# A fourth seven-product pair in the first down trip of each chunk, with its weight sums made at the end of up

## The chip, the cores and the metric

One core of one Trainium2 chip runs the whole kernel in one launch. The metric is the device time of one execution in microseconds (us). Each version is timed in several runs and the median is given.

## The reference, cut to what matters

A decoder layer: a token-mixing sub-layer with three branches, then a squared-ReLU MLP, on 256 tokens of 2048 channels, all float32. The change touches only the MLP, and there only its second matrix product:

```python
D_MODEL, SEQ, D_FF = 2048, 256, 4 * 2048
h = rmsnorm(x, norm_ffn_g[l])
x = x + jnp.square(jax.nn.relu(h @ w_up[l])) @ w_down[l]
return rmsnorm(x, final_g)
```

## The kernel before

**Precision.** Each float32 weight is split in a high part `w_hi` (made by ScalarE, L607) and a low part `w_lo` = weight - high (VectorE, L890), and so are the activations. A product is then three matmuls: high x high, low x high, high x low.

**Slabs.** Weights stream from memory in slabs of 512 KB, 128x1024 elements. SyncE issues the loads into 8 raw buffers (`w_raw`). The split forms lie in a ring of 4 (`w_hi`, `w_lo`). In step k of the program ScalarE and VectorE prepare slab k + 3 while TensorE multiplies slab k.

**Chunks.** The MLP is cut in 4 chunks of 2048 hidden channels. A chunk is the phase `up` (4 trips of 8 slabs; a trip has two groups n = 0 and 1 of 4 slabs, so the trip's last step is k = 7) and the phase `down` (2 trips of 16 slabs; the two groups n = 0 and 1 are two blocks of 512 output columns, i = 0 to 7 is the place along the hidden channels). Chunk 0 and chunk 3 are written out, chunks 1 and 2 are a loop.

**The end of a group of up.** When a group's last slab has been multiplied, ScalarE copies half of the sums out of PSUM (`second`, L816), VectorE adds the other half (L1438), multiplies by the row scale (L1440, which counts the semaphore `evac_done`), squares the ReLU (L1487), and after the last step of a trip also makes four sums of activations for the seven-product form (`a_sums`, L961 to L966) and the low parts (L1493, L970). Group n uses the PSUM banks 4 + 2n and 5 + 2n, and so does group n of `down`. Therefore the first slab of a group of down (i = 0) waits until the group of up that held the same banks has been taken out:

```python
if i == 0:
    pe.wait_ge(evac_done, g - 1)
```

**Seven products in place of eight.** Two slabs with the same i, (0, i) and (1, i), hold a 2x2 arrangement of weight blocks. Multiplied plainly they take 2 x 12 matmuls of 512 columns (`products_as`, L1559 to L1561). As a Strassen-Winograd product (`products_quad`, L1608 to L1610) they take 7 x 3 = 21. This needs four sums of weight blocks, made by VectorE in `forms_first` (one instruction of 128x1024, L901) and `forms_second` (two of 128x512, L908, L911), their high parts by ScalarE (`forms_hi`, two of 128x1024, L613, L615) and their low parts by VectorE (`forms_lo`, two of 128x1024, L917). In return one block of the second slab needs no split of its own: only half of it is split (L605, L887). The sums of activations for i = 1, 3, 5, 7 are all made at the end of the four up trips (`a_forms[0]` to `[3]`); before the change a_forms[0] is made and not used in down.

**The order.** `order_of` gives the order of slabs in a trip, `quads` says at which steps a seven-product pair begins: (6, 10, 14). The sums of the pair at step q are made in step q - 4 (`forms_first`), q - 3 (`forms_second`), q - 2 and q - 1 (high and low parts). Each engine runs its instructions in the order of the program; within a step of VectorE that order is `forms_second`, `lo`, `forms_first`, `forms_lo`, then the end of a group. `walk` says which trips are loops.

Of the kernel before, what the change touches and what calls it, by code (L numbers as in the profile page):

```python
# [51 lines left out]
LOOKAHEAD = 3  # L52
# [4 lines left out]
KDOWN = D // DROWS  # L57
# [43 lines left out]
PH = plan()  # L101
# [7 lines left out]


PAIR = [(0, 0), (0, 1), (1, 0), (1, 1), (0, 2), (1, 2), (0, 3), (1, 3), (0, 4), (1, 4), (0, 5), (1, 5)]
PAIR_ENDS = {False: [(0, 6), (1, 6), (0, 7), (1, 7)], True: [(0, 6), (0, 7), (1, 6), (1, 7)]}
P_BANK = {"P1": 0, "P6": 1, "P7": 2, "P5": 3}
T1, T3, T2, T4 = range(4)
# [2 lines left out]
MIX_QUADS, GATE_QUADS = 3, 6  # L117
# [3 lines left out]
def last_trip(ph, c, t):  # L121

    return ph.name == "down" and isinstance(c, int) and c == CHUNKS - 1 and isinstance(t, int) and t == ph.trips - 1
# [6 lines left out]
def opening(ph, c, t):  # L130

    return ph.name == "glu" and isinstance(t, int) and t == 0


def order_of(ph, c, t):

    if opening(ph, c, t):
        return [(n, i, KFULL) for n, i in OPENING]
    if ph.name == "A":
        return [(n, i, KDOWN) for n, i in PAIR + PAIR_ENDS[False]] + ph.slabs[16:]  # L140
    if not (ph.name == "down" or ph.name == "mix" and t == 0):
        return ph.slabs
    return [(n, i, KDOWN) for n, i in PAIR + PAIR_ENDS[last_trip(ph, c, t)]]


def quads(ph, c, t):

    if ph.name == "A" or ph.name == "mix" and t == 0:
        return (6, 10, 14)
    if ph.name != "down":  # L150
        return ()
    return (6,) if last_trip(ph, c, t) else (6, 10, 14)


def quad_of(ph, c, t, k):

    at = quads(ph, c, t).index(k)
    if ph.name == "A":
        return t * 3 + at
    return GATE_QUADS + at if ph.name == "mix" else c * (3 * PH["down"].trips) + t * 3 + (at + GATE_QUADS + MIX_QUADS)  # L160


def pair_of(ph, c, t):
# [11 lines left out]
def trip_behind(ph, c, t):  # L175

    if ph.name in ("mix", "down") and t:
        return ph, c, t - 1
    if ph.name == "up" and isinstance(t, int) and not (isinstance(c, int) and c == 0):
        return PH["down"], c - 1, PH["down"].trips - 1  # L180
    return None

# [26 lines left out]
WARM_GAP = 3  # L209


def walk(eng, body):

    def loop(name, c=0, first=0):
        with eng.Fori(first, PH[name].trips) as t:
            body(PH[name], c, t)

    body(PH["glu"], 0, 0)
    loop("glu", first=1)
    for t in range(PH["short"].trips):  # L220
        body(PH["short"], 0, t)
    body(PH["kv"], 0, 0)
    for t in range(PH["q"].trips):
        body(PH["q"], 0, t)
    body("v tokens", 0, 0)
    for t in range(PH["B"].trips):
        body(PH["B"], 0, t)
    for t in range(PH["C"].trips):
        body(PH["C"], 0, t)
    for t in range(PH["A"].trips):  # L230
        body(PH["A"], 0, t)
    for t in range(PH["mix"].trips):
        body(PH["mix"], 0, t)
    def chunk(c):
        body(PH["up"], c, 0)
        loop("up", c, first=1)
        for t in range(PH["down"].trips):
            body(PH["down"], c, t)

    chunk(0)  # L240
    with eng.Fori(1, CHUNKS - 1) as c:
        chunk(c)
    chunk(CHUNKS - 1)
# [21 lines left out]
def build(nc, x, norm_mix_g, w_in, gate_b, conf_dw, conf_ln_g, conf_ln_b, w_conf_out, sconv_w,  # L265
# [5 lines left out]
    with ctx:  # L271
# [123 lines left out]
        t_raw, t_two, t_hi, t_lo = sem("t_raw"), sem("t_two"), sem("t_hi"), sem("t_lo")  # L395
# [46 lines left out]
        def half_rows(slab, a):  # L442

            return wide_rows(slab)[:, a, :]
# [146 lines left out]
        def _(act):  # L591
            def hi(ph, c, t, k):

                s = slab_of(ph, c, t, k)
                if isinstance(s, int) and s + LOOKAHEAD >= TOTAL:
                    return
                ahead = k + LOOKAHEAD

                raw = raw_slot(ph, t, ahead)
                act.wait_ge(raw_full[raw], raw_count(ph, c, t, ahead))  # L600
                if not (isinstance(s, int) and s == 0):
                    act.wait_ge(slab_used, s)
                q = ahead % RING
                if ahead - 1 in quads(ph, c, t):
                    act.activation(half_rows(w_hi[:, q], 1), half_rows(w_raw[:, raw], 1), ACT.Copy).then_inc(hi_done, 1)  # L605
                else:
                    act.activation(w_hi[:, q], w_raw[:, raw], ACT.Copy).then_inc(hi_done, 1)  # L607

            def forms_hi(ph, c, t, k):

                if k + 2 in quads(ph, c, t):
                    act.wait_ge(t_raw, quad_of(ph, c, t, k + 2) * 2 + 2)
                    act.activation(forms_of(ph)[:, 0, 2:4, :], w_sums[:, 2:4, :], ACT.Copy).then_inc(t_hi, 1)  # L613
                if k + 1 in quads(ph, c, t):
                    act.activation(forms_of(ph)[:, 0, 0:2, :], w_sums[:, 0:2, :], ACT.Copy).then_inc(t_hi, 1)  # L615

            def first_product(ph, c, t, k):
# [250 lines left out]
                        if k == 12:  # L868
                            closing_squares()

            walk(act, trip)
            act.wait_ge(rstd3, 2)
            act.wait_ge(y_gain, 2 * NBLK)
            act.activation(yg_tok[:, 1, W2:], yg_tok[:, 1, W2:], ACT.Copy, scale=tok_stat[:, 2, 1:2]).then_inc(scaled[3], 1)
# [3 lines left out]
        def _(dve):  # L878
            def lo(ph, c, t, k):
                s = slab_of(ph, c, t, k)  # L880
                if isinstance(s, int) and s + LOOKAHEAD >= TOTAL:
                    return
                q, raw = (k + LOOKAHEAD) % RING, raw_slot(ph, t, k + LOOKAHEAD)

                dve.wait_ge(hi_done, s + (LOOKAHEAD + 1))
                if k + LOOKAHEAD - 1 in quads(ph, c, t):
                    dve.tensor_tensor(half_rows(w_lo[:, q], 1), half_rows(w_raw[:, raw], 1),  # L887
                                      half_rows(w_hi[:, q], 1).bitcast(F32), ALU.subtract).then_inc(lo_done, 1)
                else:
                    dve.tensor_tensor(w_lo[:, q], w_raw[:, raw], w_hi[:, q].bitcast(F32), ALU.subtract).then_inc(lo_done, 1)  # L890

            def forms_first(ph, c, t, k):

                x, y = raw_slot(ph, t, k), raw_slot(ph, t, k + 1)
                quad = quad_of(ph, c, t, k)
                if not (isinstance(quad, int) and quad == 0):
                    dve.wait_ge(t_lo, quad * 2)
                dve.wait_ge(raw_full[x], raw_count(ph, c, t, k))
                dve.wait_ge(raw_full[y], raw_count(ph, c, t, k + 1))
                left = w_raw[:, x:x + 2, 0:2, :].rearrange("p s k b -> p s (k b)")  # L900
                dve.tensor_tensor(w_sums[:, T1:T3 + 1, :], wide_rows(w_raw[:, y]), left, ALU.subtract).then_inc(t_raw, 1)  # L901

            def forms_second(ph, c, t, k):

                x, y = raw_slot(ph, t, k), raw_slot(ph, t, k + 1)
                quad = quad_of(ph, c, t, k)
                dve.wait_ge(t_raw, quad * 2 + 1)
                dve.tensor_tensor(w_sums[:, T2, :], half_rows(w_raw[:, y], 1), w_sums[:, T1, :],  # L908
                                  ALU.subtract).then_inc(t_two, 1)
                dve.wait_ge(t_two, quad + 1)  # L910
                dve.tensor_tensor(w_sums[:, T4, :], half_rows(w_raw[:, x], 1), w_sums[:, T2, :],  # L911
                                  ALU.subtract).then_inc(t_raw, 1)

            def forms_lo(ph, c, t, k, part):
                dve.wait_ge(t_hi, quad_of(ph, c, t, k) * 2 + part + 1)
                two = slice(2, 4) if part == 0 else slice(0, 2)
                dve.tensor_tensor(forms_of(ph)[:, 1, two, :], w_sums[:, two, :], forms_of(ph)[:, 0, two, :].bitcast(F32),  # L917
                                  ALU.subtract).then_inc(t_lo, 1)
# [369 lines left out]
            def trip(ph, c, t):  # L1288
# [4 lines left out]
                for k in range(ph.nslabs):  # L1293
# [10 lines left out]
                    if opening(ph, c, t) and k == 5:  # L1304
# [1 line left out]
                        dve.reciprocal(mix_stat[:, 3, :], mix_stat[:, 2, :]).then_inc(inv1, 1)  # L1306
                        dve.wait_ge(inv1, 1)
                        spread_diagonal(diag1)
                    if k + 3 in quads(ph, c, t):
                        forms_second(ph, c, t, k + 3)  # L1310
                    if k == 15 and paired(ph, c, t) and ph.name != "A":
                        corner_sums(ph, c, t)
                    lo(ph, c, t, k)
                    if k == 0 and trip_behind(ph, c, t):
                        token_sums(*trip_behind(ph, c, t))
                    if k + 4 in quads(ph, c, t):
                        forms_first(ph, c, t, k + 4)
                    if k + 2 in quads(ph, c, t):
                        forms_lo(ph, c, t, k + 2, 0)
                    if k + 1 in quads(ph, c, t):  # L1320
                        forms_lo(ph, c, t, k + 1, 1)
                    n, i, size = order_of(ph, c, t)[k]
                    s, g, ends = slab_of(ph, c, t, k), group_of(ph, c, t, n), i == size - 1
                    if ph.name == "down" and not last_trip(ph, c, t):
# [10 lines left out]
                    if opening(ph, c, t):  # L1335
# [10 lines left out]
                        if k == 6:  # L1346
# [3 lines left out]
                            n, i, size = order_of(ph, c, t)[5]  # L1350
# [39 lines left out]
                    if ph.name == "short":  # L1390
# [4 lines left out]
                        first = sum(CONV_SHORT[m] for m in range(k))  # L1395
# [26 lines left out]
                    if ph.name == "C":  # L1422
                        at = t * ph.nslabs + k
# [79 lines left out]
                            dve.tensor_tensor(y_tok[:, b, cols], acc[:, bank(ph, n) + b, :], y_tok[:, b, cols],  # L1503
                                              ALU.add).then_inc(done, 1)

            walk(dve, trip)


        @block.tensor
# [356 lines left out]
```

## Time and profile before

| | |
|---|---|
| median of 3 runs | 1507.08 us (1505.09 to 1507.33) |
| the profiled execution, its own time | 1505.21 us |
| its span in the trace | 1503.4 us |
| TensorE busy | 1491.5 us, 99% of the span |
| VectorE busy | 1246.7 us, 83% |
| ScalarE busy | 780.2 us, 52% |
| DMA engines | 61.1% |
| granted TensorE clock | 0.999 |

The span is what the trace covers; some 1.8 us of the execution's own time lie around it. TensorE is busy in the whole span, so the end moves with what TensorE has to do and with what it has to wait for.

### The profile page before, as it was taken

The page shows a single profiled execution, that of the slowest core. Times are in us where ns is not written, and L with a number is a line of the kernel's source. Part 1 is how long each engine was busy: PE and PEld are TensorE (multiplying, and loading weights), DVE is VectorE, ACT ScalarE, POOL GpSimd, SP SyncE. Part 2 cuts the span into 40 slices and gives each one's busy share as a digit, 9 for nine tenths or more (in the row PEclk, how much of TensorE's full clock was granted, in tenths as well). Part 3 has the DMA queues.
Part 4 walks back from the last instruction along what each step waited for, and adds up shares of the span by engine and source line. Part 5 has one row for each costly group of instructions (what it writes and reads, how often), then busy time and mean ns, then how long its engine had stood idle before and what let it go on. Part 6 is the DMA issues. An engine that isn't in the chain of part 4 may idle for free.

```text
span 1503.4 us, 21159 instructions
## 1 busy us (share of the span) xinstructions
PE 1491.5 (99%) x7574; PEld 1260.7 (84%) x7574; DVE 1246.7 (83%) x1670; ACT 780.2 (52%) x979; POOL 2.0 (0%) x11
## 2 busy tenths in 40 slices
PE   8999999999999999999999999999999999999998
PEld 7888888888888888888888888888888888888886
DVE  6668889988889879998976779977898779987897
ACT  6444444465554456556565455545555545544554
POOL 0000000000000000000000000000000000000000
PEclk9999999999999999999999999999999999999999
DMA  9666665665556666665655656655666566656662
GB/s 310 194 184 188 193 195 183 204 185 177 177 175 198 194 192 197 207 215 185 195 185 182 195 173 217 205 191 171 210 201 205 168 206 204 194 180 209 209 203 90
DMA packets 210028, 291.11 MB, mean 194 GB/s; under 512 B 9276, under 2 KB 129156, under 8 KB 209827
## 3 DMA queue, kind: packets, MB, share of 16 engines
q1 hardware_dynamic: 209954, 290.14, 61.1%
q8 instruction: 45, 0.74, 0.2%
q14 instruction: 29, 0.23, 0.0%
HBM read 287.48 MB, written 2.10 MB: 193 GB/s over the span
## 4 chain that ended last, share of the span: by engine, by line
PE 99%; DVE 0%; ACT 0%; DMA 0%; issue 0%; SPq 0%; DVEq 0%
PE acc L1539 27%; PE acc L1559 14%; PE acc L1560 14%; PE acc L1561 14%; PE acc L1537 13%; PE acc L1609 3%; PE acc L1608 3%; PE acc L1610 3%; PE acc L1532 2%; PE acc L1636 1%; PE acc L1534 1%; PE acc L1702 0%; PE acc L1722 0%; PE acc L1580 0%; PE acc L1579 0%; PE acc L1578 0%
## 5 line engine op out<-in xcount | busy, mean ns | idle before, releaser
L607 ACT ACTIVATE w_hi<-w_raw 128x1024 fp32r<-128x1024 f32 x502 | 524.5, 1057 | 437.5 <-PE acc L1561 237.2
L890 DVE TENSOR_TENSOR w_lo<-w_raw,w_hi 128x1024 fp32r<-128x1024 f32 x502 | 605.8, 1221 | 139.4 <-ACT w_hi L607 135.7
L1539 PE MATMUL acc<-h_hl,w_hi 128*128 128x512 f32 x1740 | 546.6, 395 | 0.0
L1537 PEld LDWEIGHTS acc<-h_hl,w_lo 128*128 128x128 f32 x1740 | 322.3, 188 | 73.1 <-issue 0.7
L1537 PE MATMUL acc<-h_hl,w_lo 128*128 128x256 f32 x1740 | 343.5, 279 | 0.4 <-DVE w_lo L1044 0.3
L1539 PEld LDWEIGHTS acc<-h_hl,w_hi 128*128 128x128 f32 x1740 | 265.2, 189 | 0.0
L1559 PE MATMUL acc<-w_hi,m_hl 128*128 128x512 f32 x424 | 165.3, 390 | 0.0
L1560 PE MATMUL acc<-w_lo,m_hl 128*128 128x512 f32 x424 | 165.0, 389 | 0.0
L1561 PE MATMUL acc<-w_hi,m_hl 128*128 128x512 f32 x424 | 165.0, 389 | 0.0
L1559 PE MATMUL acc<-w_hi,h_hl 128*128 128x512 f32 x336 | 132.2, 394 | 0.0
L1561 PE MATMUL acc<-w_hi,h_hl 128*128 128x512 f32 x336 | 130.9, 389 | 0.0
L1560 PE MATMUL acc<-w_lo,h_hl 128*128 128x512 f32 x336 | 130.8, 389 | 0.0
L1098 DVE SCALAR_TENSOR_TENSOR conv<-glu,par,conv 128x256 f32<-128x256 f32 x240 | 108.9, 479 | 1.4
L1561 PEld LDWEIGHTS acc<-w_hi,m_hl 128*128 128x128 f32 x424 | 79.6, 188 | 16.5
L1559 PEld LDWEIGHTS acc<-w_hi,m_hl 128*128 128x128 f32 x424 | 79.6, 188 | 16.5
L1560 PEld LDWEIGHTS acc<-w_lo,m_hl 128*128 128x128 f32 x424 | 79.6, 188 | 16.4
L816 ACT ACTIVATE second<-acc 128x512 f32<-128x512 f32 x58 | 34.7, 599 | 101.7 <-PE acc L1539 101.7
L1438 DVE TENSOR_TENSOR pair<-acc,second 128x512 f32<-128x512 f32 x54 | 37.2, 690 | 54.4 <-ACT second L816 54.3
L1559 PEld LDWEIGHTS acc<-w_hi,h_hl 128*128 128x128 f32 x336 | 63.1, 188 | 14.1 <-issue 1.3
L1561 PEld LDWEIGHTS acc<-w_hi,h_hl 128*128 128x128 f32 x336 | 63.1, 188 | 13.3
L1560 PEld LDWEIGHTS acc<-w_lo,h_hl 128*128 128x128 f32 x336 | 63.1, 188 | 12.7
L917 DVE TENSOR_TENSOR w_forms<-w_sums,w_forms 128x1024 fp32r<-128x1024 f32 x50 | 60.9, 1219 | 0.0
(270 smaller groups left out, 1651.8 us busy)
## 6 DMA issues: line engine op xcount, KB each, us to landing
w_raw<-in_w_in SPq DMA_DIRECT2D x197, 512.0 KB, 4.3
w_raw<-in_w_up SPq DMA_DIRECT2D x128, 512.0 KB, 4.3
w_raw<-in_w_down SPq DMA_DIRECT2D x128, 512.0 KB, 4.5
w_raw<-in_w_mix_out SPq DMA_DIRECT2D x32, 512.0 KB, 3.9
w_raw<-in_w_sconv_out SPq DMA_DIRECT2D x16, 512.0 KB, 3.8
w_raw<-in_w_attn_out SPq DMA_DIRECT2D x16, 512.0 KB, 3.8
w_raw<-in_w_conf_out SPq DMA_DIRECT2D x16, 512.0 KB, 4.0
bias_row<-in_gate_b SPq DMA_DIRECT2D x10, 256.0 KB, 4.1
```

The source lines that it names most:

```text
L607: act.activation(w_hi[:, q], w_raw[:, raw], ACT.Copy).then_inc(hi_done, 1)
L890: dve.tensor_tensor(w_lo[:, q], w_raw[:, raw], w_hi[:, q].bitcast(F32), ALU.subtract).then_inc(lo_done, 1)
L917: dve.tensor_tensor(forms_of(ph)[:, 1, two, :], w_sums[:, two, :], forms_of(ph)[:, 0, two, :].bitcast(F32), ALU.subtract).then_inc(t_lo, 1)
L1098: dve.scalar_tensor_tensor(dst, src, w, dst, ALU.mult, ALU.add).then_inc(step, 1)
L1537: pe.matmul(*narrow[m], start=False, stop=False)
L1539: last = pe.matmul(*wide[m], start=False, stop=final)
L1559: pe.matmul(acc[:, b + m, :], h_h, hi[:, a, :], start=first, stop=False)
L1560: pe.matmul(acc[:, b + m, :], h_h, lo[:, a, :], start=False, stop=False)
L1561: last = pe.matmul(acc[:, b + m, :], h_l, hi[:, a, :], start=False, stop=final)
L1608: pe.matmul(acc[:, at, :], rows[0], columns[0], start=start, stop=False)
L1609: pe.matmul(acc[:, at, :], rows[0], columns[1], start=False, stop=False)
L1610: return pe.matmul(acc[:, at, :], rows[1], columns[0], start=False, stop=stop)
```

## The change

In the first down trip (t = 0) of each chunk the order of slabs begins with `EARLY`, and a fourth seven-product pair starts at step 2, with i = 1. Its sums would fall in the steps -2 to 1. The new functions `quad_at`, `sums_at` and `last_sums_at` put them one to two steps earlier, into the last trip of up: `forms_first` in step 5, `forms_second` in step 6, all high and low parts in step 7. For this ScalarE and VectorE have the last up trip written out in place of being the last pass of the loop over t (`split=True`).

```diff
 PAIR = [(0, 0), (0, 1), (1, 0), (1, 1), (0, 2), (1, 2), (0, 3), (1, 3), (0, 4), (1, 4), (0, 5), (1, 5)]
+EARLY_AT = 2
+EARLY = [(0, 0), (1, 0), (0, 1), (1, 1)]
@@ order_of
+    if ph.name == "down" and t == 0:
+        return [(n, i, KDOWN) for n, i in EARLY + PAIR[4:] + PAIR_ENDS[False]]
@@ quads
+    if t == 0:
+        return (EARLY_AT, 6, 10, 14)
     return (6,) if last_trip(ph, c, t) else (6, 10, 14)
+
+
+def quad_at(ph, c, t, k):
+
+    if k >= ph.nslabs and ph.name == "up" and isinstance(t, int) and t == ph.trips - 1:
+        ph, t, k = PH["down"], 0, k - ph.nslabs
+    return (ph, c, t, k) if k in quads(ph, c, t) else None
+
+
+def sums_at(ph, c, t, k):
+
+    ahead = quad_at(ph, c, t, k + 1)
+    if ahead and ahead[3] == EARLY_AT:
+        return ahead
+    at = quad_at(ph, c, t, k)
+    return None if at and at[3] == EARLY_AT else at
+
+
+def last_sums_at(ph, c, t, k):
+
+    ahead = sums_at(ph, c, t, k + 1)
+    if ahead and ahead[3] == EARLY_AT:
+        return ahead
+    at = sums_at(ph, c, t, k)
+    return None if at and at[3] == EARLY_AT else at
@@ walk
-        loop("up", c, first=1)
+        loop("up", c, first=1, last=1 if split else 0)
+        if split:
+            body(PH["up"], c, PH["up"].trips - 1)
@@ scalar, forms_hi
-                if k + 2 in quads(ph, c, t):
+                if sums_at(ph, c, t, k + 2):
...
-                if k + 1 in quads(ph, c, t):
+                if last_sums_at(ph, c, t, k + 1):
@@ vector, trip
-                    if k + 3 in quads(ph, c, t):
-                        forms_second(ph, c, t, k + 3)
+                    if sums_at(ph, c, t, k + 3):
+                        forms_second(*sums_at(ph, c, t, k + 3))
...
-                    if k + 4 in quads(ph, c, t):
-                        forms_first(ph, c, t, k + 4)
-                    if k + 2 in quads(ph, c, t):
-                        forms_lo(ph, c, t, k + 2, 0)
-                    if k + 1 in quads(ph, c, t):
-                        forms_lo(ph, c, t, k + 1, 1)
+                    if sums_at(ph, c, t, k + 4):
+                        forms_first(*sums_at(ph, c, t, k + 4))
+                    if sums_at(ph, c, t, k + 2):
+                        forms_lo(*sums_at(ph, c, t, k + 2), 0)
+                    if last_sums_at(ph, c, t, k + 1):
+                        forms_lo(*last_sums_at(ph, c, t, k + 1), 1)
```

The instructions move at two places. On VectorE, the steps 4 to 7 of an up trip before the change, which in chunk 0 is the body of a loop (`lo` of four slabs, then the end of the group; the register rows belong to the loop):

```order
L885 REGISTER_ALU
L890 TENSOR_TENSOR w_lo<-w_raw,w_hi 128x1024 [waits hi_done]
L885 REGISTER_ALU
L890 TENSOR_TENSOR w_lo<-w_raw,w_hi 128x1024 [waits hi_done]
L885 REGISTER_ALU
L890 TENSOR_TENSOR w_lo<-w_raw,w_hi 128x1024 [waits hi_done]
L885 REGISTER_ALU
L890 TENSOR_TENSOR w_lo<-w_raw,w_hi 128x1024 [waits hi_done]
L1437 REGISTER_ALU [waits slab_used]
L1438 TENSOR_TENSOR pair<-acc,second 128x512 [waits half_copied]
L1439 REGISTER_ALU
L1440 TENSOR_TENSOR pair<-pair,rstd 128x512 [waits half_sum]
```

The same steps of the last up trip after it (L923 is the former L890, L1471 and L1473 the former L1438 and L1440, L934 to L944 and L950 the former L901 to L911 and L917):

```order
L923 TENSOR_TENSOR w_lo<-w_raw,w_hi 128x1024 [waits hi_done] x2
L934 TENSOR_TENSOR w_sums<-w_raw 128x1024 [waits raw_full3,raw_full2,t_lo]
L941 TENSOR_TENSOR w_sums<-w_raw,w_sums 128x512 [waits t_raw]
L944 TENSOR_TENSOR w_sums<-w_raw,w_sums 128x512 [waits t_two]
L923 TENSOR_TENSOR w_lo<-w_raw,w_hi 128x1024 [waits hi_done] x2
L950 TENSOR_TENSOR w_forms<-w_sums,w_forms 128x1024 [waits t_hi] x2
L1471 TENSOR_TENSOR pair<-acc,second 128x512 [waits half_copied,slab_used]
L1473 TENSOR_TENSOR pair<-pair,rstd 128x512 [waits half_sum]
```

Five instructions of the weight sums now stand between the low parts of the slabs and ahead of the last group's end. On TensorE, the first three slabs of down before (each slab is 12 matmuls; the left-out rows are further matmuls without a wait):

```order
L1559 MATMUL acc<-w_hi,m_hl 128x512 [waits evac_done,lo_done,hid_lo]
L1560 MATMUL acc<-w_lo,m_hl 128x512
...
L1559 MATMUL acc<-w_hi,m_hl 128x512 [waits lo_done,hid_lo]
...
L1559 MATMUL acc<-w_hi,m_hl 128x512 [waits evac_done,lo_done,hid_lo]
L1560 MATMUL acc<-w_lo,m_hl 128x512
```

And after, the first two slabs and the first products of the added pair (L1592 is the former L1559, L1641 the former L1608):

```order
L1592 MATMUL acc<-w_hi,m_hl 128x512 [waits evac_done,lo_done,hid_lo]
...
L1592 MATMUL acc<-w_hi,m_hl 128x512 [waits evac_done,lo_done,hid_lo]
...
L1641 MATMUL acc<-w_hi,m_hl 128x512 [waits lo_done,hid_lo]
...
L1641 MATMUL acc<-w_forms,m_hl 128x512 [waits t_lo]
...
L1641 MATMUL acc<-w_hi,a_forms 128x512 [waits f_lo,lo_done]
```

The second wait on `evac_done`, the one for the last group of up, has moved from down's third slab to its second.

## Rows read from the trace of the kernel before

**Rows 1.** The page: the chain that ended last, by engine.

```profile
PE 99%; DVE 0%; ACT 0%; DMA 0%; issue 0%; SPq 0%; DVEq 0%
```

**Rows 2.** Waits of TensorE: the two longest of four; us, times, longest.

```profile
PE acc L1636 <- POOL mask L584: 2.4, 1, 2.4
PE acc L1532 <- DVE h_hl L1052: 1.1, 1, 1.1
```

**Rows 3.** Timeline of TensorE, chunk 0, up to down: start, length, instruction.

```profile
894.66 0.39 PE L1559 MATMUL acc<-w_hi,m_hl 128*128 128x512 f32 x1
...
897.39 0.39 PE L1559 MATMUL acc<-w_hi,m_hl 128*128 128x512 f32 x1
...
900.12 0.39 PE L1559 MATMUL acc<-w_hi,m_hl 128*128 128x512 f32 x1
```

**Rows 4.** Timeline of VectorE, last up trip of chunk 0; idle time before in brackets.

```profile
884.41 0.69 DVE L1438 TENSOR_TENSOR pair<-acc,second 128x512 f32<-128x512 f32 x1 [1.18 <-ACT second L816]
...
888.31 3.50 DVE L890 TENSOR_TENSOR w_lo<-w_raw,w_hi 128x1024 fp32r<-128x1024 f32 x3
893.17 1.23 DVE L890 TENSOR_TENSOR w_lo<-w_raw,w_hi 128x1024 fp32r<-128x1024 f32 x1 [1.36 <-ACT w_hi L607]
895.58 0.69 DVE L1438 TENSOR_TENSOR pair<-acc,second 128x512 f32<-128x512 f32 x1 [1.18 <-ACT second L816]
896.30 0.69 DVE L1440 TENSOR_TENSOR pair<-pair,rstd 128x512 f32<-128x512 f32 x1
```

**Rows 5.** Timeline of TensorE: first matmul of a seven-product pair and of what follows it.

```profile
911.00 0.39 PE L1608 MATMUL acc<-w_hi,m_hl 128*128 128x512 f32 x1
...
915.75 0.39 PE L1559 MATMUL acc<-w_hi,m_hl 128*128 128x512 f32 x1
```

**Rows 6.** Timeline of VectorE: the weight sums of the pair at step 6.

```profile
904.02 1.22 DVE L901 TENSOR_TENSOR w_sums<-w_raw 128x1024 f32<-128x1024 f32 x1
905.28 0.69 DVE L908 TENSOR_TENSOR w_sums<-w_raw,w_sums 128x512 f32<-128x512 f32 x1
906.01 0.69 DVE L911 TENSOR_TENSOR w_sums<-w_raw,w_sums 128x512 f32<-128x512 f32 x1
906.62 1.22 DVE L890 TENSOR_TENSOR w_lo<-w_raw,w_hi 128x1024 fp32r<-128x1024 f32 x1
907.75 0.68 DVE L887 TENSOR_TENSOR w_lo<-w_raw,w_hi 128x512 fp32r<-128x512 f32 x1
```

**Rows 7.** Timeline of ScalarE: a high part of weight sums.

```profile
906.73 1.07 ACT L613 ACTIVATE w_forms<-w_sums 128x1024 fp32r<-128x1024 f32 x1 [0.29 <-DVE w_sums L911]
```

**Rows 8.** Timeline of VectorE: first up trip of chunk 1, which is written out.

```profile
989.70 0.69 DVE L1438 TENSOR_TENSOR pair<-acc,second 128x512 f32<-128x512 f32 x1 [1.09 <-ACT second L816]
...
993.50 3.50 DVE L890 TENSOR_TENSOR w_lo<-w_raw,w_hi 128x1024 fp32r<-128x1024 f32 x3 [0.26 <-ACT w_hi L607]
...
1000.86 0.69 DVE L1438 TENSOR_TENSOR pair<-acc,second 128x512 f32<-128x512 f32 x1 [1.18 <-ACT second L816]
...
1005.80 3.50 DVE L890 TENSOR_TENSOR w_lo<-w_raw,w_hi 128x1024 fp32r<-128x1024 f32 x3 [0.26 <-ACT w_hi L607]
```

**Rows 9.** Timelines of TensorE and VectorE: the same boundary in chunk 3.

```profile
1411.52 0.39 PE L1559 MATMUL acc<-w_hi,m_hl 128*128 128x512 f32 x1
...
1412.43 0.69 DVE L1438 TENSOR_TENSOR pair<-acc,second 128x512 f32<-128x512 f32 x1 [1.18 <-ACT second L816]
```

**Rows 10.** Timeline of all engines: TensorE after a wait for VectorE.

```profile
6.54 0.88 DVE L1052 SCALAR_TENSOR_TENSOR h_hl<-acc,par,h_hl 128x256 fp32r<-128x256 f32 x2
...
7.48 0.74 PE L1532 MATMUL acc<-h_hl,w_hi 128*128 128x512 f32 x2 [1.09 <-DVE h_hl L1052]
...
8.53 0.62 PE L1539 MATMUL acc<-h_hl,w_hi 128*128 128x512 f32 x2
```

**Rows 11.** Window 0 to 7 us: busy per engine (x instructions), clock, DMA, GB/s.

```profile
0.00:7.00 7.00, 3.98 (x17) 3.51 (x17) 1.28 (x4) 3.33 (x6) 1.98 (x11) 1.00 0.57 180
```

**Rows 12.** Loads issued from 860 to 915 us: KB, median us to landing.

```profile
w_raw<-in_w_down SPq DMA_DIRECT2D x18, 512.0 KB, 4.9
```

More of the change, by code:

```diff
@@ L159, in quad_of @@
         return t * 3 + at
-    return GATE_QUADS + at if ph.name == "mix" else c * (3 * PH["down"].trips) + t * 3 + (at + GATE_QUADS + MIX_QUADS)
+    return GATE_QUADS + at if ph.name == "mix" else c * 7 + t * 4 + (at + GATE_QUADS + MIX_QUADS)
 def pair_of(ph, c, t):
@@ L178, in trip_behind @@
         return ph, c, t - 1
-    if ph.name == "up" and isinstance(t, int) and not (isinstance(c, int) and c == 0):
+    if ph.name == "up" and isinstance(t, int) and t == 0 and not (isinstance(c, int) and c == 0):
         return PH["down"], c - 1, PH["down"].trips - 1
@@ L209, with walk, loop @@
 WARM_GAP = 3
-def walk(eng, body):
-    def loop(name, c=0, first=0):
-        with eng.Fori(first, PH[name].trips) as t:
+def walk(eng, body, split=False):
+    def loop(name, c=0, first=0, last=0):
+        with eng.Fori(first, PH[name].trips - last) as t:
             body(PH[name], c, t)
@@ L603, in hi @@
                 q = ahead % RING
-                if ahead - 1 in quads(ph, c, t):
+                if quad_at(ph, c, t, ahead - 1):
                     act.activation(half_rows(w_hi[:, q], 1), half_rows(w_raw[:, raw], 1), ACT.Copy).then_inc(hi_done, 1)
@@ L609, in forms_hi @@
             def forms_hi(ph, c, t, k):
-                if k + 2 in quads(ph, c, t):
-                    act.wait_ge(t_raw, quad_of(ph, c, t, k + 2) * 2 + 2)
+                if sums_at(ph, c, t, k + 2):
+                    act.wait_ge(t_raw, quad_of(*sums_at(ph, c, t, k + 2)) * 2 + 2)
                     act.activation(forms_of(ph)[:, 0, 2:4, :], w_sums[:, 2:4, :], ACT.Copy).then_inc(t_hi, 1)
-                if k + 1 in quads(ph, c, t):
+                if last_sums_at(ph, c, t, k + 1):
                     act.activation(forms_of(ph)[:, 0, 0:2, :], w_sums[:, 0:2, :], ACT.Copy).then_inc(t_hi, 1)
@@ L869, in trip @@
                             closing_squares()
-            walk(act, trip)
+            walk(act, trip, split=True)
             act.wait_ge(rstd3, 2)
@@ L885, in lo @@
                 dve.wait_ge(hi_done, s + (LOOKAHEAD + 1))
-                if k + LOOKAHEAD - 1 in quads(ph, c, t):
+                if quad_at(ph, c, t, k + LOOKAHEAD - 1):
                     dve.tensor_tensor(half_rows(w_lo[:, q], 1), half_rows(w_raw[:, raw], 1),
@@ L1504, in trip @@
                                               ALU.add).then_inc(done, 1)
-            walk(dve, trip)
+            walk(dve, trip, split=True)
         @block.tensor
```

## The prediction, on record before the changed kernel was run

> **What bounds the kernel now.** I read the chain that ended last first: 99% of it is TensorE [rows 1]. Then TensorE's own waits: there are four in the whole span, the two longest 2.4 and 1.1 us, both at the start [rows 2]. So in the four chunks TensorE never waits. A matmul less is time gained, and a wait that appears is time lost, to the full amount. The question is what slack the boundary from up to down has, since the change takes its VectorE work from there. For this I read the timelines of TensorE and VectorE side by side.
>
> In chunk 0 down starts on TensorE at 894.66 us, its second slab at 897.39, its third at 900.12: 2.73 us for a slab, 5.46 for two [rows 3]. On VectorE the low parts of the steps 4 to 6 start at 888.31, then it idles 1.36 us until the high part of step 7's slab is there, then 1.18 us until ScalarE's copy of the last group; the add starts at 895.58, the multiply that counts `evac_done` at 896.30 and takes 0.69, so it ends at 896.99 [rows 4]. The third slab of down, which has to wait for it, starts 3.1 us later. The second slab would have been only 0.4 us after it. The same place in chunk 3 reads the same: down starts at 1411.52, the add at 1412.43, 0.91 us behind as against 0.92 [rows 9, 3, 4]; I take all four chunks alike.
>
> **Part 1, fewer matmuls.** A seven-product pair starts at 911.00 and what follows at 915.75: 4.75 us [rows 5]. Two plain slabs take 5.46 [rows 3]. One pair more in each of 4 chunks: 4 x 0.71 = 2.8 us less on TensorE. No more can come of the change, since no other matmul goes.
>
> **Part 2, the wait that moves.** `EARLY` puts slab (1, 0) second in place of third. Its first matmul needs the PSUM banks of up's last group. So TensorE asks for that `evac_done` at 897.39 in place of 900.12. If nothing else changed there would be 0.4 us to spare.
>
> **Part 3, VectorE's added instructions ahead of it.** Per chunk: one sum of 1.22 us, two of 0.69 [rows 6], two low parts of the size of a 128x1024 subtract, in return one low part is cut in half (0.68 for 1.22). All five stand ahead of the last group's add in VectorE's own order, as the order rows above show. The engine's starts follow each other at these distances: three low parts busy 3.50 us in all at 1.22 each, so 1.14 from one to the next [rows 4]; first sum to second 1.26, second to third 0.73, third to the next low part 0.61, and from that on 1.13 [rows 6]. I take 1.14 for the low parts of the sums.
>
> Start of the train: in the loop the low part of step 4 starts 3.90 us after the add of the group before (884.41 to 888.31 [rows 4]). In a trip that is written out it is 3.80 (989.70 to 993.50 [rows 8]). The last up trip is now written out, so I start it at 888.2. Then: low part of step 5 at 889.35, first sum 890.5, second 891.75, third 892.5, low part of step 6 at 893.1, of step 7 at 894.2, low parts of the sums at 895.4 and 896.5, the add at 897.65, the multiply 0.72 later at 898.4, its end at 899.1.
>
> Does anything else on this train wait? The high part of step 7's slab was there at 893.17 [rows 4], before 894.2. The third sum is there at 893.2; ScalarE then makes the two high parts, 1.07 us each [rows 7], by 894.3 and 895.3, each over 1 us ahead of its low part, and its copy of the last group comes next, at about 896, ahead of 897.65. The first sum reads two raw slabs earlier than ScalarE does. The later of them may be loaded once step 0 of this trip is past, which was before 884.41 [rows 4]; a load lands in 4.9 us [rows 12], so by 889.3, ahead of 890.5. So the train is bound by VectorE alone.
>
> TensorE's second slab of down then starts not at 897.39 but behind 899.1. Starting again costs something: after VectorE's end at 7.42 (6.54 + 0.88) TensorE began at 7.48, and two matmuls took 0.74 us where they take 0.62 in a stream [rows 10]. That is 0.06 and 0.12 us, so a wait of 1.7 becomes a loss of 1.85 a chunk, 7.4 us in four. The idle 2.5 us that VectorE had here cover only half of what is added.
>
> Bounds for this term. Below: no cost of restart and 0.2 us more saved by code without loop registers, 1.5 a chunk. Above: each of the seven instructions between the low part of step 5 and the add starts only when its predecessor has ended, 0.08 us more each, 2.3 to 2.4 a chunk. The row with 3.50 us for three at 1.22 [rows 4] shows the overlap plainly, so I stay with 1.85. The Trainium skill ("VectorE: DVE Perf Modes", The DRAIN you can't avoid) says that the next operation does not start until the pipe has emptied, and that waits between operations make no difference to it; taken as a full duration from start to start that would be the upper bound, and the sum would be about +6.6 us in place of +4.6. The trace shows starts closer than durations, and it decides.
>
> **Part 4, what is late next.** Behind the add on VectorE stand the ReLU square, the sums and low parts of activations, then the half low part of the pair's second slab. TensorE needs that one at its third product, 2 x 3 matmuls into the pair. From the add to the low part after the end of the trip it is 4.94 us, of which 0.26 is a wait for a high part of full size [rows 8]; a half one is 0.4 shorter. So it starts at about 902.4 and ends at 903.1. TensorE: 899.2 + 2.73 + 6 x 0.227 (2.73 / 12) = 903.3. I cost it at nothing; with the slack at 0.2 us, up to 0.3 a chunk is possible, 1.2 in all. The later low parts have 2 us and more, since VectorE's place against TensorE recovers in the idle time that it has in each plain slab. The pair's own sums are complete before the add, so they cannot hold TensorE longer than the banks do. ScalarE's added two high parts (2.1 us) lie in its idle time.
>
> **Sum.** -2.8 + 7.4 = +4.6 us, +0.31%. Against the profiled execution (1505.21 with 1503.4 in the span) this is 1509.8. That execution lies at the lower end of the three runs, whose median is 1507.08, 1.9 above it. I set the base half way, 1506.15, and predict 1510.8 us.
>
> **Rivals.**
> *The wait is hidden (not slower).* If the add of the last group could still start by 895.9 (897.39 less the 1.47 us that add, multiply and release take), TensorE would not wait and the whole 2.8 us would be gained: 1503.4, within 0.2%. It decides at 0.35 us of delay. For it speaks the idle time of VectorE in steps 5 to 7 (2.5 us), against it that 4.9 us are put there (1.26 + 0.73 + 0.61 + 2 x 1.14). Chance 0.10.
> *Half hidden.* The train starts earlier or runs closer than the rows say and the wait is 0.7 to 1.4 us: 0 to +2.8 us, 1506 to 1509, still within 0.2%. Chance 0.12.
> *Two waits.* The banks as above and in addition the half low part of Part 4 late by 0.3 us or more in each chunk, or the pair at step 6 late: +6.5 to +9 us, 1513 to 1515. For it speaks the slack of 0.2 us, against it the idle time behind it. Chance 0.09.
> *The clock falls.* If TensorE's clock went from 2.4 to 1.2 GHz after each wait, a slab at half speed would add 2.7 us: +15 us, 1521. Against it: from 0 to 7 us TensorE was busy only 3.98 us, and its granted clock was 1.00 [rows 11]. The Trainium skill ("TensorE: Matmul & The Clock Gate", Part 1) makes the clock depend on recent activity and lets idleness bring the low level back; by it a wait could cost more than its length. No stretch of this trace shows the low level. Chance 0.02.
> My forecast itself: 0.67.
>
> **How the numbers follow.** What a measurement of this kernel can tell is about 0.2%, 3.0 us. The forecast gives 3.2 us (4 x 1.5 - 2.8) to 7.8 (4 x 2.35 - 2.8 + 1.2), on a base between 1505.2 and 1507.1: its own range is 1508.4 to 1514. The full range takes in the half hidden case from 1507 and the lower part of two waits, to 1514.5; it leaves out the hidden wait, the clock and the edges, under 2 in 10. Slower: forecast and the two worse cases, 0.77 with a little taken off for the edge at 3.0. Same: hidden and half hidden, 0.20. Faster by over 0.2% would need more than 2.8 us: 0.03, for what the base may hide.
>
> **What would show it.** In the new profile TensorE's waits should list four of about 1.7 us, at the second slab of down, released by VectorE's multiply (`pair`); 12 matmuls fewer; VectorE's five added instructions in one unbroken train ahead of the last group's add, which starts some 2.1 us later than before against up's last slab. If the waits are released by `w_lo` or `w_forms`, Part 4 was wrong. If no waits are listed and the time is 2.8 us lower, the train was shorter than its rows. If the waits are 1.7 us and the time is much higher still, something outside this boundary changed, such as code of the trip now written out.

## The result and the profile after

The changed kernel takes 1510.76 us (median of 8 runs, 1509.87 to 1511.96), the kernel before 1506.24 us in as many runs on the same chip (1505.09 to 1507.44). The ratio is 1.0031, 95% interval 1.0023 to 1.0040: slower by 0.3%. Predicted were 1510.8 us and slower. Among the runs of the experiments below, one of e1 took 2505.46 us and one of e3 1853.46 us, at a mean granted clock of 0.557 and 0.753 where all others have 0.992 or more; they stand outside the ratios.

The profiled execution took 1511.88 us, with a span of 1510.1. The three longest of TensorE's five waits in it, with total us, times and the longest (compare [rows 2]):

```profile
PE acc L1592 <- DVE pair L1473: 6.2, 4, 1.6
PE acc L1669 <- POOL mask L617: 2.6, 1, 2.6
PE acc L1565 <- DVE h_hl L1085: 0.8, 1, 0.8
```

One new line, four times: a plain down matmul waits for VectorE's multiply of the last group. The page's busy times and the chain that ended last:

```profile
PE 1491.9 (99%) x7562; PEld 1260.1 (83%) x7562; DVE 1262.4 (84%) x1690; ACT 786.0 (52%) x987; POOL 2.0 (0%) x11
...
PE 95%; DVE 3%; issue 1%; ACT 1%; DMA 0%; SPq 0%; DVEq 0%; ACTq 0%
```

TensorE has 12 matmuls fewer (7562 for 7574), VectorE 20 instructions more, and the chain, 99% of which was TensorE [rows 1], now runs through VectorE for 3%. The timeline of VectorE at the end of up in chunk 0 (start, length, instruction) answers to [rows 4]; everything in this execution stands some 2.0 us later by a cause in its first 12 us, told at the end:

```profile
890.18 2.36 DVE L923 TENSOR_TENSOR w_lo<-w_raw,w_hi 128x1024 fp32r<-128x1024 f32 x2 [0.26 <-ACT w_hi L640]
892.46 1.22 DVE L934 TENSOR_TENSOR w_sums<-w_raw 128x1024 f32<-128x1024 f32 x1
893.71 0.69 DVE L941 TENSOR_TENSOR w_sums<-w_raw,w_sums 128x512 f32<-128x512 f32 x1
894.43 0.69 DVE L944 TENSOR_TENSOR w_sums<-w_raw,w_sums 128x512 f32<-128x512 f32 x1
895.04 2.35 DVE L923 TENSOR_TENSOR w_lo<-w_raw,w_hi 128x1024 fp32r<-128x1024 f32 x2
897.32 2.35 DVE L950 TENSOR_TENSOR w_forms<-w_sums,w_forms 128x1024 fp32r<-128x1024 f32 x2
899.59 0.68 DVE L1471 TENSOR_TENSOR pair<-acc,second 128x512 f32<-128x512 f32 x1
900.30 0.69 DVE L1473 TENSOR_TENSOR pair<-pair,rstd 128x512 f32<-128x512 f32 x1
```

Behind the 0.26 us at the first row no idle time stands in brackets up to the multiply's end at 900.99: one unbroken train. The timeline of TensorE at the same place:

```profile
896.65 0.39 PE L1592 MATMUL acc<-w_hi,m_hl 128*128 128x512 f32 x1
...
901.14 0.47 PE L1592 MATMUL acc<-w_hi,m_hl 128*128 128x512 f32 x1 [1.59 <-DVE pair L1473]
...
903.97 0.39 PE L1641 MATMUL acc<-w_hi,m_hl 128*128 128x512 f32 x1
```

Down starts at 896.65; its second slab, due 2.73 us later at 899.38 (the distance of [rows 3]), starts at 901.14, and the pair at 903.97, where 902.11 was due. That is a loss of 1.76 at the wait and 1.86 with the slower restart. (The profile lists 1.59 us for this wait, as it counts from the end that it gives the last matmul, 0.17 us behind the next one's due start.) Down of chunk 0, both its trips, from down's start to the next start of up, took 82.97 us before and takes 84.15. Up of the chunks 1 and 2 takes 89.3 us in both kernels, and that of chunk 0 takes 90.64, so writing out its last trip cost nothing.

### The profile page after: what moved, and what is told of

Same layout as the page of the kernel before. It is cut to its first block, busy times and chain, and to the rows that moved or that the text cites. A ratio compares the mean times of both kernels' runs of the same rounds, so it can differ in the third digit from the quotient of the medians.

```text
span 1510.1 us, 21085 instructions
## 1 busy us (share of the span) xinstructions
PE 1491.9 (99%) x7562; PEld 1260.1 (83%) x7562; DVE 1262.4 (84%) x1690; ACT 786.0 (52%) x987; POOL 2.0 (0%) x11
## 4 chain that ended last, share of the span: by engine, by line
PE 95%; DVE 3%; issue 1%; ACT 1%; DMA 0%; SPq 0%; DVEq 0%; ACTq 0%
PE acc L1572 25%; PE acc L1592 14%; PE acc L1593 14%; PE acc L1594 14%; PE acc L1570 12%; PE acc L1642 4%; PE acc L1641 4%; PE acc L1643 4%; PE acc L1565 2%; PE acc L1669 1%; PE acc L1567 1%; DVE w_lo L923 1%; DVE w_forms L950 0%; PE acc L1735 0%; DVE pair L1473 0%
## 5 line engine op out<-in xcount | busy, mean ns | idle before, releaser
L923 DVE TENSOR_TENSOR w_lo<-w_raw,w_hi 128x1024 fp32r<-128x1024 f32 x498 | 601.2, 1221 | 135.1 <-ACT w_hi L640 132.1
L1592 PE MATMUL acc<-w_hi,m_hl 128*128 128x512 f32 x392 | 153.2, 391 | 6.2 <-DVE pair L1473 6.2
L1593 PE MATMUL acc<-w_lo,m_hl 128*128 128x512 f32 x392 | 152.6, 389 | 0.0
L1594 PE MATMUL acc<-w_hi,m_hl 128*128 128x512 f32 x392 | 152.6, 389 | 0.0
L1592 PE MATMUL acc<-w_hi,h_hl 128*128 128x512 f32 x336 | 132.2, 394 | 0.0
L1592 PEld LDWEIGHTS acc<-w_hi,m_hl 128*128 128x128 f32 x392 | 73.6, 188 | 23.0 <-issue 4.0
L1594 PEld LDWEIGHTS acc<-w_hi,m_hl 128*128 128x128 f32 x392 | 73.6, 188 | 15.4
L1593 PEld LDWEIGHTS acc<-w_lo,m_hl 128*128 128x128 f32 x392 | 73.6, 188 | 15.0
L1471 DVE TENSOR_TENSOR pair<-acc,second 128x512 f32<-128x512 f32 x54 | 37.2, 689 | 49.8 <-ACT second L849 49.6
L1592 PEld LDWEIGHTS acc<-w_hi,h_hl 128*128 128x128 f32 x336 | 63.1, 188 | 14.1 <-issue 1.3
L950 DVE TENSOR_TENSOR w_forms<-w_sums,w_forms 128x1024 fp32r<-128x1024 f32 x58 | 70.3, 1217 | 0.0
```

Of the source, the lines that this page charges most:

```text
L1592: pe.matmul(acc[:, b + m, :], h_h, hi[:, a, :], start=first, stop=False)
L1593: pe.matmul(acc[:, b + m, :], h_h, lo[:, a, :], start=False, stop=False)
L1594: last = pe.matmul(acc[:, b + m, :], h_l, hi[:, a, :], start=False, stop=final)
```

## The experiments

Times are compared with the kernel before on the same chip. From here on, "the trip" is TensorE's time from the start of down in chunk 0 to the start of up in chunk 1; it covers both trips of down, although the expectations of e6 and e7 call it the first. It is free of what happens in the first microseconds of an execution.

**e1, the order alone.** In the kernel before:

```diff
+EARLY = [(0, 0), (1, 0), (0, 1), (1, 1)]
+    if ph.name == "down" and t == 0:
+        return [(n, i, KDOWN) for n, i in EARLY + PAIR[4:] + PAIR_ENDS[False]]
```

> Only the order of the first four slabs of down is changed in the kernel before; no fourth pair, no sums moved. My theory: the wait for the banks is asked for 2.73 us earlier, but the multiply that ends it is over 0.4 us before that, so nothing waits: 1506.2 us, within 0.3 us of before, and no wait of TensorE inside the chunks. Rival, that moving the wait costs by itself: four waits of 0.3 us or more at the second slab of down, 1507.5 us or above.

Ratio 0.9998 (0.9989 to 1.0007); no wait inside the chunks; the trip 82.97 us, as before. Asking for the banks a slab earlier costs nothing as long as VectorE's train is as it was.

**e2, sums and order without the seven products.** The two slabs are multiplied plainly (24 matmuls, as before) and the second slab's parts are made whole; the weight sums are made and read by nothing:

```diff
+def products_at(ph, c, t):
+    return tuple(k for k in quads(ph, c, t) if k != EARLY_AT)
...
-                    if k in quads(ph, c, t):
+                    if k in products_at(ph, c, t):
                         products_quad(ph, c, t, k)
```

> All of the change but the seven products: the two slabs at steps 2 and 3 are multiplied plainly and the second one's low and high parts are made whole; the sums are made and not used. My theory: the loss without the gain, +7.4 us, 1513.6 us (1512.5 to 1514.5), four waits of 1.6 to 1.8 us released by VectorE's multiply of the last group. Rival, that part of the loss lies in the products of the pair or in waits for its sums: less than +6 us.

Ratio 1.0041 (1.0028 to 1.0053), +6.2 us with an interval of 4.2 to 8.0; the median of five runs, 1512.38, lies just under the range that was expected, and the interval leaves the rival open. The lowest runs of both kernels are 7.4 us apart (1512.33 and 1504.95). The trace is sharper: the trip takes 84.82 us, 1.85 above before, and TensorE's only wait inside the chunks is

```profile
PE acc L1599 <- DVE pair L1480: 6.2, 4, 1.6
```

the same as in the changed kernel. So the loss, 4 x 1.85 = 7.4 us, is all there without the pair. Against the changed kernel's 84.15 the pair gives 0.67 a chunk.

**e3, the last group ahead of the sums' low parts.** In the changed kernel, on VectorE (the same two calls are left out at their former place):

```diff
                         total(pair[n][:, :, :], both(rstd))
+                        if sums_at(ph, c, t, k + 2):
+                            forms_lo(*sums_at(ph, c, t, k + 2), 0)
+                            forms_lo(*last_sums_at(ph, c, t, k + 1), 1)
                         dve.wait_ge(evac_done, g + 1)
```

> The changed kernel with VectorE's two low parts of the sums put behind the last group's add and multiply. My theory: the multiply ends 2.3 us earlier, before TensorE asks for the banks, so the wait at the second slab goes; but the half low part of the pair's second slab comes no earlier, and TensorE, which no longer loses time, reaches the third product 1.8 us earlier: four new waits of about 1.2 us released by that low part, 1508.7 us (1508 to 1509.5). Rival, that the banks were the only limit: no waits, 1503.4 us.

Ratio 1.0031 (1.0018 to 1.0044), the trip 84.13 us: nothing gained, where I had expected 2 us. The wait did move as expected:

```profile
PE acc L1644 <- DVE w_lo L920: 6.2, 4, 1.6
```

It is now at the pair's third product. The expectation had it at 1.2 us, 0.4 too short. The timeline of VectorE shows why:

```profile
892.83 2.35 DVE L923 TENSOR_TENSOR w_lo<-w_raw,w_hi 128x1024 fp32r<-128x1024 f32 x2
895.54 0.69 DVE L1471 TENSOR_TENSOR pair<-acc,second 128x512 f32<-128x512 f32 x1 [0.36 <-ACT second L849]
896.27 0.69 DVE L1473 TENSOR_TENSOR pair<-pair,rstd 128x512 f32<-128x512 f32 x1
896.88 2.35 DVE L950 TENSOR_TENSOR w_forms<-w_sums,w_forms 128x1024 fp32r<-128x1024 f32 x2
...
902.20 0.68 DVE L920 TENSOR_TENSOR w_lo<-w_raw,w_hi 128x512 fp32r<-128x512 f32 x1
```

With the add this early, VectorE meets ScalarE's copy, which stands behind both high parts of the sums, and idles 0.36 us; the half low part behind it all is later by that. It ends at 902.88, and TensorE's third product, due at 901.29 (a matmul's distance behind the one at 901.06), starts at 902.93. Two limits lie one behind the other here: the banks, and the half low part. Removing the first alone returns nothing.

**e4, the half low part as well.** The kernel of e3 with:

```diff
                             forms_lo(*last_sums_at(ph, c, t, k + 1), 1)
+                            lo(PH["down"], c, 0, 0)
...
+                            if sums_at(ph, c, t, k + 2):
+                                hi(PH["down"], c, 0, 0)
                             j = t * 2 + n
```

and the two calls left out of step 0 of down.

> The kernel of e3, and the half high and low part of the pair's second slab are put ahead of the ReLU square and the sums of activations, on ScalarE and VectorE. My theory: the half low part is ready 1.8 us before the third product, the next low part 1 us before its slab; no wait in the chunks, and the gain of the 12 matmuls remains: 1503.4 us, 0.19% below before. Rival, that the pair or the trip written out cost something else: 1505 us or above, or a new wait for the low part of down's fifth slab.

Ratio 0.9992 (0.9984 to 1.0001): the four waits are gone, none is listed in the chunks, but the median is 1504.45 us where 1503.4 was expected, and the trip takes 82.70 us, 0.27 below before in place of 0.70. The view of waits does not show what is left, the timeline of TensorE does:

```profile
910.66 0.39 PE L1649 MATMUL acc<-w_hi,m_hl 128*128 128x512 f32 x1
910.88 0.39 PE L1650 MATMUL acc<-w_lo,m_hl 128*128 128x512 f32 x1
911.11 0.39 PE L1651 MATMUL acc<-w_hi,m_hl 128*128 128x512 f32 x1
911.52 0.50 PE L1649 MATMUL acc<-w_forms,m_hl 128*128 128x512 f32 x1
911.86 0.40 PE L1650 MATMUL acc<-w_forms,m_hl 128*128 128x512 f32 x1
```

These are the first products of the next pair, at step 6. Matmuls start every 0.23 us, but here 0.41 and 0.34 us pass. Ahead of the fourth the program waits for the sums' low part (which the fifth reads), and VectorE has only just finished it, at 911.46:

```profile
903.64 2.36 DVE L926 TENSOR_TENSOR w_lo<-w_raw,w_hi 128x1024 fp32r<-128x1024 f32 x2 [0.26 <-ACT w_hi L640]
...
910.24 1.22 DVE L953 TENSOR_TENSOR w_forms<-w_sums,w_forms 128x1024 fp32r<-128x1024 f32 x1
```

**e6, one high part earlier.** The kernel of e4 with `hi(PH["down"], c, 0, 1)` as well ahead of ScalarE's two activation copies.

> The kernel of e4 with the high part of down's fifth slab put ahead of ScalarE's two activation copies. In e4 the first down trip takes 82.70 us from down's start to the next up, 0.43 above what the pair's 21 matmuls leave; TensorE hesitates at the pair of step 6, where VectorE's low part of the sums ends at 911.46, and VectorE had stood 0.26 us idle at 903.64 for that high part. My theory: VectorE's train is late by this much; the trip falls by about 0.26 us to 82.44, 1 us in four: 0.1 to 0.15% below before in all. Rival, that the hesitation is something else: unchanged, 0.08% below before.

Ratio 0.9984 (0.9975 to 0.9993), the trip 82.33 us: 0.37 below e4, more than the 0.26 us of idle time taken away. In e4 the lateness at the fourth matmul was 0.18 us (0.41 less 0.23), and the slower pace behind it the rest: the first 12 matmuls of this pair took 3.06 us there and take 2.74 here.

**e7, two more moves.** The kernel of e6 with the following, each call left out at its former place:

```diff
+                    if ph.name == "down" and t == 0 and k == 4:
+                        forms_lo(*sums_at(ph, c, t, k + 2), 0)
                     if not (ph.name == "down" and t == 0 and k == 0):
                         lo(ph, c, t, k)
...
                         act.activation(second[:, :, :], acc[:, b:b + 2, SEQ:], ACT.Copy).then_inc(half_copied, 1)
+                    if ph.name == "up" and last_sums_at(ph, c, t, k + 1):
+                        act.activation(w_forms[:, 0, 0:2, :], w_sums[:, 0:2, :], ACT.Copy).then_inc(t_hi, 1)
```

> The kernel of e6, and two more moves: in step 4 of down VectorE makes the first low part of the sums ahead of the half low part, and at the end of up ScalarE makes its copy of the last group ahead of the second high part of the sums (VectorE stood 0.36 us idle for that copy in e4). My theory: nothing is late at the pair of step 6, the trip takes 82.27 us, 2.8 us below before, 1503.4 us on before's 1506.2 (ratio 0.9981 to 0.9983). Rival, that a wait appears at the half low part or elsewhere: the trip stays at 82.4 or above.

1502.56 us against 1505.57, ratio 0.9976 (0.9966 to 0.9985): faster than both kernels by a little, and the trip takes 82.29 us, 0.68 below before, as expected. The ratio flatters it somewhat: eight of its nine runs are of the lower of the two groups told at the end, 11 of the 21 of the kernel before. The lowest runs are 2.7 us apart (1502.30 and 1504.99), 4 x 0.68. Against e6 the trip shows 0.04 us, and the lowest runs 0.2. The windows of 888 to 905 us, with the busy times of TensorE, its weight loads, VectorE and ScalarE, then granted clock, DMA share and GB/s, first the changed kernel, then e7:

```profile
888.00:905.00 17.00, 15.40 (x79) 12.80 (x79) 15.56 (x22) 9.94 (x13) 0.00 (x0) 1.00 0.48 163
```

```profile
888.00:905.00 17.00, 17.00 (x85) 14.35 (x84) 16.58 (x22) 10.54 (x13) 0.00 (x0) 1.00 0.46 157
```

VectorE has 1690 instructions in either kernel; only their order differs. (e7 is 2.2 us ahead by then, so the windows cut the train at different places.) In e7 TensorE is busy throughout.

**e5, one of the added instructions doubled.** In the changed kernel, per chunk, the first sum is made once more into memory that nothing reads:

```diff
+                if ph.name == "down" and k == EARLY_AT:
+                    dve.tensor_tensor(gates_y[:, :, :], wide_rows(w_raw[:, y]), left, ALU.subtract)
```

> The changed kernel with one VectorE instruction more per chunk: the first sum of weight blocks (128x1024, 1.22 us) is made once more into memory that nothing reads, in the train ahead of the last group's add. My theory: the train has no idle time, so the dose comes through in full: four waits of 2.7 to 2.8 us in place of 1.6, 4 x 1.14 = 4.6 us above the changed kernel, 1515.4 us (ratio to before 1.0061). Rival, that something else ends the wait (ScalarE's copy or a load): less than 3 us above.

Waits as expected, time not. Ratio 1.0085 (1.0071 to 1.0098), 1517.58 us, some 2 us more than expected:

```profile
PE acc L1594 <- DVE pair L1475: 10.8, 4, 2.7
```

10.8 us for 6.2: the added instruction lengthens the four waits by 4.6 us in all, its full price. The rest is the clock. The timeline of TensorE behind the first of the four waits:

```profile
900.25 0.77 PE L1594 MATMUL acc<-w_hi,m_hl 128*128 128x512 f32 x1 [2.73 <-DVE pair L1475]
900.82 0.63 PE L1595 MATMUL acc<-w_lo,m_hl 128*128 128x512 f32 x1
901.25 0.63 PE L1596 MATMUL acc<-w_hi,m_hl 128*128 128x512 f32 x1
...
903.38 0.45 PE L1595 MATMUL acc<-w_lo,m_hl 128*128 128x512 f32 x1
903.67 0.40 PE L1596 MATMUL acc<-w_hi,m_hl 128*128 128x512 f32 x1
```

A matmul every 0.43 us for some 3 us, where they come every 0.23. The windows around it, and those behind the waits of chunks 1 and 2, columns as above:

```profile
893.00:900.00 7.00, 4.52 (x22) 3.47 (x20) 6.93 (x8) 2.66 (x4) 0.00 (x0) 1.00 0.54 195
900.00:904.00 4.00, 3.75 (x10) 3.01 (x11) 3.69 (x9) 2.71 (x4) 0.00 (x0) 0.57 0.02 8
904.00:908.00 4.00, 4.00 (x19) 3.28 (x18) 3.28 (x3) 1.21 (x3) 0.00 (x0) 1.00 0.65 205
...
1076.00:1080.00 4.00, 3.69 (x11) 3.00 (x12) 3.72 (x9) 2.48 (x4) 0.00 (x0) 0.70 0.06 22
...
1252.00:1256.00 4.00, 3.54 (x16) 2.92 (x16) 3.71 (x9) 2.32 (x4) 0.00 (x0) 1.00 0.09 34
```

The granted clock is 0.57 in 900 to 904 us, mostly the low level of 1.2 GHz, and 1.00 on either side. In chunk 1 the clock falls too, but only 1.3 us behind the restart, after five matmuls at the full pace:

```profile
1076.31 0.50 PE L1594 MATMUL acc<-w_hi,m_hl 128*128 128x512 f32 x1 [2.65 <-DVE pair L1475]
...
1077.57 0.62 PE L1596 MATMUL acc<-w_hi,m_hl 128*128 128x512 f32 x1
```

In chunks 2 and 3 the wait was as long (2.65 and 2.73 us) and the clock stayed at 1.00. The trips show the price: 86.82 and 86.83 us in chunks 0 and 1, 85.24 in chunk 2, that is 1.6 us for a fallen clock. 4.6 + 2 x 1.6 = 7.8 us above the changed kernel; measured are 7.5 between the lowest runs of both (1517.40 and 1509.87). One run of e5 took 1523.47 us, with a mean granted clock of 0.992 where the other five have 0.996; it has no trace, but more falls of the clock would fit it.

## Why the prediction was right

*Part 1*, 0.71 us a chunk gained: measured 0.67 from e2 against the changed kernel, 0.68 from e7 against before (three matmuls at a distance of 0.227).

*Part 2*, the moved wait costs nothing by itself: e1, trip unchanged.

*Part 3*, VectorE's train. Predicted were 1.85 us lost a chunk, measured 1.85 in e2 (84.82 less 82.97). The spacing read from [rows 4, 6] held to 0.04 us: the train from the low part of step 4 to the add took 9.41 us (890.18 to 899.59), worked out as 9.45. That the sum is exact has some luck in it: the multiply ended 4.34 us behind down's start where 4.44 was worked out, but TensorE began 0.15 us behind that end, not 0.06. The overlap of 0.08 us between neighbours is there in the added instructions too: two low parts of the sums take 2.35 us in all at 1.22 each. The prediction had set it against the Trainium skill ("VectorE: DVE Perf Modes", The DRAIN you can't avoid). That section also says that "a next op that is not held starts earlier", which the prediction left out. The trace agrees with the lower price.

*Part 4* costed the half low part at nothing. In the changed kernel that holds: it started at 904.09, ended at 904.77, and the third product at 905.33 did not wait for it. But it was only hidden by the wait before it. e3 showed that it is the second limit, of the same size, and e4 that behind it came a third, of 0.4 us, at the pair of step 6, to which I had given 2 us and more of slack, for a TensorE that loses 1.85 first.

*The base, and luck.* Half way between 1505.2 and 1507.1 was 1506.15; eight runs gave 1506.24. No run of either kernel lies near its median: the runs form two groups 2 us apart (last section), four of eight in either group for both kernels, so both medians fell half way between. That 1510.8 was met to 0.04 us is luck. The part that was worked out, +4.6 us, stands against 4.8 between the lowest runs (1509.87 and 1505.09) and 4 x 1.18 = 4.7 from the trip. The prediction's own range has a slip: 1507.1 + 7.8 is 1514.9 and not 1514; the measured time is inside either.

*The rivals.* The hidden wait and the half hidden one did not occur: the train has no idle time in it. Two waits did not occur in the changed kernel. The clock did not fall after its waits of 1.6 us, but it did after two of four waits of 2.7 us in e5. The mechanism of that rival is real in this kernel, and the changed kernel is some 1.1 us of VectorE work away from it. Its price there was 1.6 us a time, not the 2.7 of a whole slab. What the prediction held against it, TensorE little busy from 0 to 7 us at a granted clock of 1.00 [rows 11], was no evidence, and that no stretch of that trace shows the low level was wrong: the column reads 1.00, but from 4.21 us on four transposes took nearly twice what the same form takes later (last section).

## What to carry to other kernels

Where one engine is busy all the time, price a saved instruction at its distance to the next one (0.23 us for a matmul to which the timeline gives 0.39), and then look for what each helper must finish by when, not at how busy it is: VectorE had 2.5 us idle in the three steps that took 4.9 us of new work, and the 2.0 us by which the last group came later against TensorE (0.92 us behind down's start before, 2.94 after) used up 0.4 us of slack and became a loss of more than twice the gain. When such a wait is removed, walk on along the helper's train to the next thing that its consumer needs; here three limits stood behind one another, and all the profit came only when the work that nobody waits for (the activations' sums and low parts of up's last group, which down first reads at step 14) went to the end of the queue. Work that lengthens a wait can cost more than its own length.

## What was not expected of the hardware

**Two groups of runs, 2 us apart, for every kernel.** The kernel before has runs at 1504.9 to 1505.6 and at 1506.8 to 1507.6 and none between, the changed one at 1509.9 to 1510.1 and at 1511.5 to 1512.0. The one run between two groups is 1513.13 us in e2. The traces place it in the first 12 us. Timeline of TensorE in the changed kernel, from an execution of the upper group:

```profile
7.39 1.22 PE L1565 MATMUL acc<-h_hl,w_hi 128*128 128x512 f32 x2 [0.79 <-DVE h_hl L1085]
...
9.26 1.05 PE L1572 MATMUL acc<-h_hl,w_hi 128*128 128x512 f32 x2
```

Two matmuls of the same form took 0.74 and 0.62 us in the kernel before, in an execution of the lower group [rows 10]. Of nine profiled executions three began this way (the changed kernel, e2, e6), all three of an upper group; the six others are of a lower group. The column of the granted clock says 1.00 for 7 to 12 us here, so that it was the clock is inferred from the lengths, which are those of the low clock in e5 (two matmuls 0.43 us apart, the last 0.63 long, make 1.06). The kernel before has such a stretch too, only shorter. In its profiled execution, of the lower group, four transposes of one form take

```profile
4.21 1.12 PE L1636 MATMUL acc<-ident,y_tok 128*128 128x128 f32 x4
...
8.99 0.60 PE L1636 MATMUL acc<-ident,y_tok 128*128 128x128 f32 x4
```

while the column says 1.00 for both. So every execution looked at seems to start slow, and the groups differ in when that ends: before the first wide matmuls at 7.5 us, or only at some 11.5. What decides between the two is open. The groups explain most of the spread of every median in this study, and why trips from the trace separate kernels that medians don't.

**The clock after a wait is not a matter of its length alone.** Waits of 2.65 to 2.73 us, at the same place of four chunks and behind a steady stream of matmuls, brought the low clock twice in four: once from the restart on, once 1.3 us behind it. No run here shows what decides it.
